# First block: attention units and recurrence heads among the tiles of the last two input products, heads turned by pairs

## What is computed

```python
proj = rmsnorm(x) @ w_in
dq, dk, dvv, mq, mk, mv, mo, mi, mf = split(proj)       # 512,512,512,256,256,512,512,4,4
# 4 differential heads: two softmax maps per head, the second subtracted with weight lam
p_diff = softmax(q0 k0) - lam * softmax(q1 k1)
o_diff = rmsnorm(p_diff @ v) * (1 - lambda_init)
# 4 recurrence (mLSTM) heads, in the kernel in parallel form over the whole sequence
hm = rmsnorm(mlstm(silu(conv(mq)), silu(conv(mk)), mv, mi, logsigmoid(mf)))
x = x + rmsnorm(concat(o_diff, hm * sigmoid(mo)) @ w_out)
x = x + rmsnorm(relu(rmsnorm(x) @ w_up)**2 @ w_down)
```

## Time and profile before

| | |
|---|---|
| median of 3 runs | 1146.79 us (1146.73 to 1147.61) |
| the profiled execution's own time | 1147.94 us |
| its span, first to last instruction | 1146.1 us |
| TensorE busy | 1120.0 us, 98% |
| VectorE, ScalarE, GpSimd busy | 791.0, 641.8, 13.2 us |
| HBM read | 182.45 MB, 160 GB/s over the span |

### The profile page before, as it was taken

How to read it: one execution, slowest core, us unless ns; L and a number is a source line. 1 busy time by engine, 2 the same in 40 slices (tenths; PEclk the granted TensorE clock), 3 DMA queues, 4 the chain that set the end, 5 groups by cost and what they waited for, 6 DMA issues and landing times.

```text
span 1146.1 us, 19220 instructions
## 1 busy us (share of the span) xinstructions
PE 1120.0 (98%) x7046; PEld 978.1 (85%) x7046; DVE 791.0 (69%) x1439; ACT 641.8 (56%) x1086; POOL 13.2 (1%) x23
## 2 busy tenths in 40 slices
PE   9998899999999999999999999999999999999998
PEld 7876789989987887888878999999876779999997
DVE  5867556555557667477674787787875756877876
ACT  5465455454456556565564665555656656655554
POOL 0000100000000000000000000000000000000000
PEclk9998899999999999999999999999999999999999
DMA  8552145555535564054622466555551514565462
GB/s 323 168 173 70 56 129 183 184 188 189 188 135 198 169 198 154 13 195 160 210 98 74 137 197 199 189 175 186 182 184 59 201 58 165 184 202 189 163 205 103
DMA packets 117037, 184.34 MB, mean 161 GB/s; under 512 B 6640, under 2 KB 70384, under 8 KB 116720
## 3 DMA queue, kind: packets, MB, share of 16 engines
q1 hardware_dynamic: 116688, 183.23, 48.8%
q10 hardware_dynamic: 288, 0.29, 0.1%
HBM read 182.45 MB, written 1.05 MB: 160 GB/s over the span
## 4 chain that ended last, share of the span: by engine, by line
PE 90%; DVE 4%; ACT 3%; issue 2%; DMA 1%; SPq 0%; DVEq 0%; ACTq 0%
PE ps L655 10%; PE ps L679 10%; PE ps L681 10%; PE ps L680 10%; PE ps L657 10%; PE ps L656 10%; PE ps L738 5%; PE ps L739 5%; PE ps L740 5%; PE ps L832 2%; PE ps L815 2%; PE ps L797 2%; PE ps L858 1%; ACT w_hi L1132 1%; DVE w_lo L1648 1%
## 5 line engine op out<-in xcount | busy, mean ns | idle before, releaser
L1648 DVE TENSOR_TENSOR w_lo<-w_stage,w_hi 128x1024 fp32r<-128x1024 f32 x336 | 403.8, 1222 | 194.3 <-ACT w_hi L1132 193.3
L1132 ACT ACTIVATE w_hi<-w_stage 128x1024 fp32r<-128x1024 f32 x336 | 349.8, 1056 | 203.0 <-PE ps L657 106.2
L679 PE MATMUL ps<-aT_hi,w_hi 128*128 128x256 f32 x992 | 282.2, 284 | 1.2 <-DVE aT_lo L1662 1.1
L680 PE MATMUL ps<-aT_lo,w_hi 128*128 128x256 f32 x992 | 281.4, 284 | 0.0
L681 PE MATMUL ps<-aT_hi,w_lo 128*128 128x256 f32 x992 | 281.4, 284 | 0.0
L655 PE MATMUL ps<-w_hi,aT_hi 128*128 128x512 f32 x480 | 191.9, 400 | 3.7 <-issue 2.2
L679 PEld LDWEIGHTS ps<-aT_hi,w_hi 128*128 128x128 f32 x992 | 190.9, 192 | 2.9 <-issue 1.3
L680 PEld LDWEIGHTS ps<-aT_lo,w_hi 128*128 128x128 f32 x992 | 191.0, 193 | 1.1
L681 PEld LDWEIGHTS ps<-aT_hi,w_lo 128*128 128x128 f32 x992 | 191.0, 193 | 0.0
L657 PE MATMUL ps<-w_hi,aT_lo 128*128 128x512 f32 x480 | 188.2, 392 | 0.0
L656 PE MATMUL ps<-w_lo,aT_hi 128*128 128x512 f32 x480 | 187.9, 391 | 0.0
(11 more groups left out here) (226 smaller groups left out, 1184.6 us busy)
## 6 DMA issues: line engine op xcount, KB each, us to landing
w_stage<-in_ffn_w_up SPq DMA_DIRECT2D x88, 512.0 KB, 4.8
w_stage<-in_a_w_qkv SPq DMA_DIRECT2D x72, 512.0 KB, 3.8
w_stage<-in_ffn_w_down SPq DMA_DIRECT2D x44, 512.0 KB, 3.5
w_stage<-in_w_up SPq DMA_DIRECT2D x32, 512.0 KB, 3.7
w_stage<-in_w_down SPq DMA_DIRECT2D x32, 512.0 KB, 4.3
w_stage<-in_w_in SPq DMA_DIRECT2D x24, 512.0 KB, 4.5
w_stage<-in_b_w_qkv SPq DMA_DIRECT2D x24, 512.0 KB, 4.3
w_stage<-in_w_out SPq DMA_DIRECT2D x8, 512.0 KB, 3.7
```

The costliest lines, as they stand in the source:

```text
L679: pe.matmul(o, wh, aT_hi[:, k, :], start=(k == 0), stop=False)
L680: pe.matmul(o, wh, aT_lo[:, k, :], start=False, stop=False)
L1132: act.activation(w_hi[:, slot, :], w_in[:, slot, :], ACT.Copy).then_inc(hi_done[slot], 1)
L1648: dve.tensor_tensor(w_lo[:, slot, :], w_in[:, slot, :], w_hi[:, slot, :].bitcast(F32), ALU.subtract).then_inc(lo_done[slot], 1)
```

## The change

In the first block:

- mv moves from in1 to mix, which gets fourteen steps over the sixteen tiles of mv and mo (`MIX_TILES`). Units start in step 0 and keep their order; heads start in step 7 (`HEAD_STEP`), one in each step.
- Queries are turned behind tile 3 of dv, keys behind tile 6. ScalarE copies both out ahead of the last passes of the silu.
- The halves 14 and 15 of in1 are made in steps 0 and 1, behind maxima and exps; the eight splits of mix follow the steps of the tiles that free their slots.
- The gates are computed in steps 2 and 3 and turned in step 4.
- GpSimd makes the product with silu (its factor goes into the ls product) and the product with lam; `pdf` is made one step later, first in VectorE's step.
- A head's output (two scaled copies, two squares) moves from VectorE to ScalarE (`head_out`). lo has two banks, m and ls one each.
- Roots are taken in three parts; heads are scaled and turned by pairs, pairs 0 and 1 in steps 11 and 13, pairs 2 and 3 among the first tiles of out1. The sigmoids and the gating, now VectorE's, stand behind the last step. The 26 small matmuls go.

In the second block the last split of each projection moves into `attention`, to step n - 1 = 7, on both engines.

The diff, cut to its core:

```diff
+        MIX_TILES = ((0,), (1, 2), (3,), (4, 5), (6,), (7,), (8,), (9,), (10,), (11,), (12,), (13,), (14,), (15,))
+        MIX_STEPS = len(MIX_TILES)
+        MIX_SPLIT = tuple(u for q in range(8) for u, tiles in enumerate(MIX_TILES) if 2 * q + 1 in tiles)
+        GATE_STEP, HEAD_STEP, FIRST_TURN, SECOND_TURN = 4, 7, 11, 13
...
-            dense_rows(S_, 0, 12, ("dv0", "dv1"))
+            dense_rows(S_, 0, 12, ("dv0", "dv1"), tiles=range(4))
...
+            dense_rows(S_, 0, 12, ("dv0", "dv1"), tiles=range(4, 7))
             turn_heads(S_, ("kt0", "kt1"), 0, 4, turned_keys)
+            dense_rows(S_, 0, 12, ("dv0", "dv1"), tiles=[7])
...
+            for u in range(MIX_STEPS):
+                for k in MIX_TILES[u]:
+                    if k < KT:
+                        dense_rows(S_, 0, 0, ("mv0", "mv1"), tiles=[k])
+                    else:
+                        dense_rows(S_, 0, 4, ("mo0", "mo1"), tiles=[k - KT])
...
+                if u == GATE_STEP:
+                    pe.wait_ge(s["gates"], at(st["in1"], "gates", 5))
+                    pe.wait_ge(*is_free(S_, "gate_m"))
+                    for j, r in enumerate((5, 7)):
+                        for t in range(TOK):
+                            last = pe.transpose(ps[:, 0, (j * 2 + t) * 4:(j * 2 + t) * 4 + 4],
+                                                gm[0:4, r, t * P:(t + 1) * P], ident[0:4, 0:4])
...
+                h = u - HEAD_STEP
+                if 0 <= h < NH1:
+
+                    if h == 0:
+                        for nm in ("mv0", "mv1"):
+                            pe.wait_ge(*is_drained(S_, nm))
+                        pe.wait_ge(s["mqk"], at(st["in1"], "mqk", 2))
                     pe.wait_ge(*is_free(S_, f"m{h}"))
-                    pe.matmul(ps[:, 6, 0:S], sel[0:4, h, :], gm[0:4, 6, :], start=True, stop=True).then_inc(full[6], 1)
+                    pe.matmul(ps[:, 2, 0:S], sel[0:4, h, :], gm[0:4, 6, :], start=True, stop=True)\
+                        .then_inc(full[2], 1)
                     r0 = (h % 2) * HD
                     pe.wait_ge(*is_free(S_, f"ls{h}"))
                     kk, qq = mqkT[r0:r0 + HD, 2 + h // 2, :], mqkT[r0:r0 + HD, h // 2, :]
-                    pe.matmul(ps[:, 7, 0:S], kk[:, 0:P], qq, start=True, stop=True)
-                    pe.matmul(ps[:, 7, S:S + P], kk[:, P:S], qq[:, P:S], start=True, stop=True).then_inc(full[7], 1)
-                if 1 <= u < len(MO_TILES):
-                    dense_rows(S_, 0, 0, ("mo0", "mo1"), tiles=MO_TILES[u])
+                    pe.matmul(ps[:, 3, 0:S], kk[:, 0:P], qq, start=True, stop=True)
+                    pe.matmul(ps[:, 3, S:S + P], kk[:, P:S], qq[:, P:S], start=True, stop=True)\
...
-                    last.then_inc(full[3], 1)
-                if h >= 1 and not odd and h <= NH1:
-                    g = h - 1
+                    last.then_inc(full[5], 1)
+                g = u - HEAD_STEP - 2
+                if 0 <= g < NH1:
+                    if g == 0:
+                        pe.wait_ge(s["const_ready"], 1)
                     pe.wait_ge(*is_free(S_, f"lo{g}"))
                     pe.wait_ge(*is_drained(S_, f"ls{g}"))
-                    w = lsm[:, g % 2, :]
-                    pe.matmul(ps[:, 6, 0:129], w[:, 0:P], vm(0)[:, g, 0:129], start=True, stop=True)
-                    pe.matmul(ps[:, 6, 256:385], w[:, P:2 * P], vm(0)[:, g, 0:129], start=True, stop=False)
-                    pe.matmul(ps[:, 6, 256:385], w[:, 2 * P:3 * P], vm(1)[:, g, 0:129],
-                              start=False, stop=True).then_inc(full[6], 1)
-
-            pe.wait_ge(*is_drained(S_, f"sA{2 * NH1 - 1}"))
-            spin(13, ps[:, 0, 0:P], ident)
-            pe.wait_ge(s["osq"], at(S_, "osq", 3))
-
-            for t in range(TOK):
...
+                    w = lsm(g)
+                    pe.matmul(ps[:, 6 + g % 2, 0:129], w[:, 0:P], vm(0)[:, g, 0:129], start=True, stop=True)
+                    pe.matmul(ps[:, 6 + g % 2, 256:385], w[:, P:2 * P], vm(0)[:, g, 0:129], start=True, stop=False)
+                    pe.matmul(ps[:, 6 + g % 2, 256:385], w[:, 2 * P:3 * P], vm(1)[:, g, 0:129],
+                              start=False, stop=True).then_inc(full[6 + g % 2], 1)
+                for j, step in enumerate((FIRST_TURN, SECOND_TURN)):
+                    if u == step:
+                        pe.wait_ge(s["osq"], at(S_, "osq", j + 1))
+                        for t in range(TOK):
+                            turn(st["turn_mix"], o_sb, None, t, range(2 * j, 2 * j + 2))
+
+            MIX = S_
             S_ = st["out1"]
             ready = after_post("post_mix")
-            dense_rows(S_, 0, 0, ("r0", "r2"), "turn_mix")
+            dense_rows(S_, 0, 0, ("r0", "r2"), "turn_mix", tiles=range(3))
+            pe.wait_ge(s["osq"], at(MIX, "osq", 3))
+            for t in range(TOK):
+                turn(st["turn_mix"], o_sb, None, t, range(4, 6))
+            dense_rows(S_, 0, 0, ("r0", "r2"), "turn_mix", tiles=[3])
+            pe.wait_ge(s["osq"], at(MIX, "osq", 4))
...
+                    if u == n - 1:
+                        split(stg, last)
...
-            splits(S_, range(12, 14))
+            split(S_, 12)
+            for j in range(2):
+                evac_q(S_, f"qt{j}", 0, 2 * j, -(HD ** -0.5))
+            split(S_, 13)
             act.wait_ge(s["conv"], at(S_, "conv", 4))
             chain.link(act.activation(u32[:], hid[:].rearrange("p a b -> p (a b)"), ACT.Exp, scale=-1.0))
+            for j in range(2):
+                evac_k(S_, f"kt{j}", 0, 2 * j, 1.0)
             chain.link(act.activation(u32[:], u32[:], ACT.Ln, bias=1.0))
             act.activation(u32[:], u32[:], ACT.Exp, scale=-1.0).then_inc(s["ecv"], 1)
-            splits(S_, range(14, 16))
-            for t in range(TOK):
-                evac_v(S_, f"dv{t}", 0, vv[:, t, 0:512], stat("rstd", 2)[:, t:t + 1])
...
+                a, b, c = (stat(nm, 16).rearrange("p (t h) -> p t h", t=TOK)[:, :, j0:j0 + heads]
+                           for nm in (name, "lno", "orstd"))
+                chain.link(act.activation(b, a, ACT.Ln, bias=EPS))
+                act.activation(c, b, ACT.Exp, scale=-0.5).then_inc(s["orstd"], 1)
+
+            def head_out(g):
+
+                act.wait_ge(s["dm"], at(S_, "dm", g + 1))
+                for t in range(TOK):
+                    last = act.activation(o_sb[:, t, 512 + g * P:512 + (g + 1) * P], ps[:, 6 + g % 2, t * S:t * S + VD], ACT.Copy,
+                                          scale=stat(f"dm{g % 2}", 2)[:, t:t + 1])
+                last.then_inc(drained[6 + g % 2], 1)
+                act.wait_ge(*is_drained(S_, f"lo{g}"))
+                for t in range(TOK):
+                    last = act.activation(xq[:, 1, t * P:(t + 1) * P], o_sb[:, t, 512 + g * P:512 + (g + 1) * P],
+                                          ACT.Square, scale=VD ** -0.5,
...
-                        last = act.activation(wmat[:, h % 2, c:c + W], lsm[:, h % 2, c:c + W], ACT.Exp, scale=-1.0,
-                                              bias=atok[:, 0, t, h:h + 1])
-                    last.then_inc(s["wm"], 1)
+                if u == 0:
+                    for t in range(TOK):
+                        evac_v(IN1, f"dv{t}", 0, vv[:, t, 0:512], stat("rstd", 2)[:, t:t + 1])
+                if u < 2:
+                    split(IN1, 14 + u)
...
+                if u == HEAD_STEP - 1:
+                    for t in range(TOK):
+                        evac_v(S_, f"mv{t}", 0, vm(t)[:, :, 0:VD], stat("rstd", 2)[:, t:t + 1],
+                               ps[:, 2 + t, :].rearrange("p (h c) -> p h c", h=NH1))
...
+            half_turned(range(2, 4))
+            for t in range(TOK):
+                act.wait_ge(*is_full(S_, f"mo{t}"))
+                act.wait_ge(s["rtok"], at(st["norm_in1"], "rtok", 1))
+                act.activation(sqb[:, t, :], ps[:, t, :], ACT.Exp, scale=stat("nrstd", 2)[:, t:t + 1])\
+                    .then_inc(drained[t], 1)
+                act.wait_ge(*is_drained(S_, f"mo{t}"))
+                chain.link(act.activation(sqb[:, t, :], sqb[:, t, :], ACT.Ln, bias=1.0))
+                act.activation(sqb[:, t, :], sqb[:, t, :], ACT.Exp, scale=-1.0).then_inc(s["sig"], 1)
+                if t == 0:
+                    act.wait_ge(s["hms"], at(S_, "hms", NH1))
+                    heads_rstd("oms", 4, 4)
+            split(S_, 7)
+            half_turned(range(4, 6))
+            half_turned(range(6, 8))
             chain.leave()
...
+            S_ = st["in1"]
+            pool.wait_ge(s["ecv"], at(S_, "ecv", 1))
+            for j in range(2):
+                pool.tensor_tensor(mqkT[:, 2 * j:2 * j + 2, :].rearrange("p a b -> p (a b)"),
+                                   hid[:, 2 * j:2 * j + 2, :].rearrange("p a b -> p (a b)"),
+                                   u32[:, j * 512:(j + 1) * 512], ALU.mult).then_inc(s["mqk"], 1)
...
+            for v, un in enumerate(units_diff()):
+                W = un["W"]
```

(59 more changed lines are left out.)

## The result

The changed kernel takes 1153.23 us (median of 5 runs, 1151.78 to 1154.35) against 1146.79 us: a ratio of 1.0055, 95% interval 1.004 to 1.0069. It is slower by 6.4 us, 1.2 us beyond the end of my range, and the interval leaves out no change. Its profiled execution took 1153.82 us with a span of 1152.0 (before: 1147.94 and 1146.1).

The account below looks back on a forecast made before the run. TensorE bounds most of the span (98% busy), engines waiting for each other the mix. Mix +0.9, clock +3, GpSimd +0.3, attention -5.1 sum to -0.9; 1147.94 - 0.9 - 1.15 (profiled run to median) = 1145.9 us, range 1136 to 1152.

Parts of the forecast that it names:

- The layout: Mix: steps laid out with row prices, engines in turn; second half of the w_out product at 140.75 against 139.82.
- out tiles 0 and 1 run from 124.05: End of the mix: start of the first two out tiles on TensorE in the laid-out steps, tile 2 to 128.6.
- the clock's term: Mix: five stalls before needed work lower TensorE's clock, 0.9 to 1.9 us each, up to 7; 3 us taken.
- The slower rival: Mix: stalls drop the clock, lengthening later stalls; +3 to +7, about 1151; decided above 4.2 us clock plus port; 30%.
- +0.9: Mix: net cost in us of the new order as laid out, the early start given back in steps and tail.
- Part two: Four attention stages: moving the last split removes a gap of 1.3 us each; -5.1 us, between -3 and -6.5.
- GpSimd: +0.3: Mix: net cost in us of products moved to GpSimd, between -1.5 and +3; a port-exclusion rule would give up to 7.8.
- The loads of weights: Mix: SP's loads of weight quarters, issued a whole turn of four slots ahead of their high halves, cost nothing.
- Layout too serial: Mix: ScalarE and VectorE run further ahead than laid out, half the turns overlap; -9.9, about 1137; 32%.
- TensorE-bound: Mix: all other work hidden behind TensorE, -22 us, with -5.1 from attention; about 1120; 6%.
- part two does nothing: Attention stages: the first units are held by something else, so no gain there; +4, 1150; 4%.
- L700 begins between 140 and 145: End of the mix: sign that the second half of the w_out product starts then, before at 139.82.

Follow-up runs that it names:

- e3: The changed kernel with keep-warm matmuls (results nobody reads, into a free bank) ahead of TensorE's waits in the mix: 1141.90 us.
- f1: e3 with ScalarE's two sigmoids ahead of head 3's output and fewer keep-warm matmuls ahead of out tile 0: 1139.90 us (one run).
- e1: The kernel before with only the attention stages' change, the last split of each projection moved behind unit 6's copies: 1138.76 us.
- e2: The changed kernel with the attention stages' change undone, so the new mix alone: 1160.65 us.
- f2: e3 with the last two in1 splits taken out of steps 0 and 1 and made earlier, fewer keep-warm matmuls: 1138.33 us (one run).
- f3: e3 with VectorE's ls product in its head's step, ahead of that step's low half, fewer keep-warm matmuls: 1139.62 us (one run).
- g1: The changed kernel with the three repairs of f1, f2 and f3 together and no keep-warm matmuls: 1141.11 us.
- f4: e1 with keep-warm matmuls ahead of five waits of the old mix: 1135.50 us.
- g4: f4 measured a second time, beside other kernels on one chip: 1136.01 us.
- g2: The changed kernel with the three repairs of f1, f2 and f3 and keep-warm matmuls: 1134.64 us.

## Why the prediction was wrong, point by point

| mark | laid out | changed kernel | e3, full clock |
|---|---|---|---|
| pd of unit 0 ends | 75.9 | 76.7 | 76.4 |
| low half ends, step 3 | 84.2 | 86.9 | 85.1 |
| step 5 | 91.7 | 96.5 | 93.0 |
| step 7 | 99.7 | 106.4 | 101.7 |
| step 9 | 110.0 | 121.7 | 112.9 |
| out tile 0 | 124.05 | 140.73 | 129.29 |
| second half, on the chain's scale | 140.75 | 155.29 | 142.83 |

**The layout was right in kind and short by 1.8 us.** With its 0.3 us for GpSimd it ends at 141.05, and e3 at 142.83. TensorE's first stall (4.5 forecast, 5.25 measured), the turns on the low half, the ls bank (3.3, 1.2, 1.9 forecast; 2.88, 1.18, 1.18 measured) are all there. It left out one wait: out tile 0 writes bank 0, which ScalarE's first sigmoid frees, and that stands behind head 3 and the second turn. So "out tiles 0 and 1 run from 124.05" failed by 5 us in e3 and by 17 in the changed kernel. The end hardly felt it, as the tail is ScalarE's, as forecast: f1 puts this wait and the idle time ahead of head 3 together at 1.5 us.

**The failed step is the clock's term: "At 0.9 to 1.9 us each that is up to 7 us", of which I took 3.** Measured 12.5. The sum was off in itself: five stalls at 0.9 to 1.9 us are 4.5 to 9.5, and the 3 that I took, as the clock would stay up for part of each, lay under that. And I had priced a single tile behind each of five stalls. What the runs show in its place is about 38 us at the lower clock between 65 us and the mark, with nearly all the work in it on the path: scores, m, ls, pd's transposes and values are as slow as tiles, VectorE and ScalarE start from them, and the waits shrank by no more than 1.3 us in return (21.9 us of stalls, 23.2 in e3).

The slower rival named the clock behind the stalls, and its point of decision was passed (12.5 against 4.2), with the price put too low at 7 plus 0.9. Its second half, a dropped clock "which makes the stall behind it longer", did not come true: together the stalls are a little shorter than at full clock. The loss grew by the number of slow matmuls, not by longer waits. I also set a mix laid out at full clock against a mark of before that had 4.4 to 5.0 us of slow clock in it, so +0.9 hid that the new order is over 7 us worse at equal clock.

**Part two was under-priced: -5.1 forecast, -8.0 measured** (e1, e2). Layer A gave 1.56 and 1.57 for my 1.3, layer B 1.7 and 3.2. Nothing returned one unit later. The extra has two parts. The 1.34 us of the row count from the end of the matmuls before, which overlaps the next start at full speed; from the four transposes ahead of the gap (456.40) to the next unit's scores (460.22) it is 3.82 us before and 2.27 after, so a gap was worth 1.55. And in b1 half of the 3.2 us is the slow clock behind the gap, 0.91 over 20 us, a term that I had not looked for there.

**GpSimd: +0.3** is neither shown nor refuted; nothing measured leaves the bounds of -1.5 to +3. (The 0.78 us of a gating product is 2.32/3 = 0.77, so the 7.8 is 7.7.) **The loads of weights** cost nothing, as taken: no high half of the mix waits for one in the trace after. **Sum**: the forecast was 11.3 us too low in the mix (9.5 clock, 1.8 layout) and 2.9 too high for attention, and 1.5 behind the norm was luck: 6.9 us, against 6.8 between the forecast and the measured change of the span (-0.9 and +5.9).

**The other rivals.** *Layout too serial* fell: in e3, even at full clock, every mark is later than laid out. *TensorE-bound* wanted the mark 22 us earlier and it came 15.5 later; *part two does nothing* fell by the 8.0 us of e1. Of the named signs, the low halves' waits, the maxima near 70, TensorE's stall (5.25 us for about 4), the slow clock between 76 and 110 (0.80) and the vanished gaps came; "L700 begins between 140 and 145" did not.

## What to carry to other kernels

When a schedule has waits of a microsecond or more on TensorE, lay it out a second time with everything behind each wait at half speed, small matmuls too, and compare at equal clock. Where the engines take turns, so that each starts from what the last one made, the waits absorb little of that loss (1.3 of 13.7 us here). Filling the waits with matmuls into a free bank is both the test and the cure (12.5 us here), and only then can the size of a single repair be read from one trace. A step that refills weights belongs behind whatever another engine waits for (part two, 8.0 us; f2, 3.1), and a product that frees a bank belongs ahead of it (f3, 1.9).

## What the hardware showed that I had not expected

- TensorE's granted clock went to its lower level (0.50, 1.2 GHz) during or soon behind every wait of 1.4 us and more in the mix of before, e1, e2 and the changed kernel (1.44 to 5.25 us), but not behind one of 1.47 us in g1 (at 122.93) nor one of 1.88 in f4 and g4. Behind a shorter one it is not each time the same: the same work with the same pause of 1.05 us behind the norm ran at a mean of 0.72 to 0.75 in four traces (before, e3, f4, g4) and at 1.00 in the ten others, which is worth 1.2 to 1.5 us of the span. Nothing that was changed goes with it: e1 has the mix of before, and the other level.
- The slow clock scatters: the nine runs of g1 lie within 7.3 us (1137.55 to 1144.88), ten of e3, kept warm, within 1.5 (1141.66 to 1143.18), g2's four within 0.4. f4's four, warm too, spread over 4.9 us, and go with their mean clock: 1133.73 us at 1.000, 1134.91 at 0.998, 1136.08 at 0.997, 1138.59 at 0.994. Only the second has a trace, so where the others were slow isn't shown.
- A product with a scalar took GpSimd 0.60 us for 128 x 128 and 0.93 for 128 x 256, where VectorE takes 0.29 and 0.35 in f4's trace.
